# Second expert table of a PEER layer: tokens as stationary operand and 512 table columns moving, in place of table columns stationary and 384 tokens moving

## The reference, cut to what matters

```python
def one_block(xb):                       # 128 tokens
    ...                                  # eidx (T, 8, 16): ids of the chosen experts; gate: softmax of their scores
    u = u_tab[eidx]
    act = gelu(einsum('thkd,td->thk', u, xb))
    return einsum('thk,thkd->td', gate * act, v_tab[eidx])
out = x + one_block(...)                 # then the final RMSNorm
```

## Time and profile before

| | us |
|---|---|
| median of three executions | 4079.37 (4070.77 to 4085.70) |
| the profiled execution | 4075.24 |
| its span in the trace | 4073.5 |
| PE busy, share of the span | 3608.8, 89% |
| DVE busy | 2568.2, 63% |
| ACT busy | 1083.2, 27% |
| POOL busy | 1355.0, 33% |
| moved by DMA | 983.08 MB, mean 241 GB/s |

### The profile page before, as it was taken

One profiled execution on the slowest core, in us unless ns is written; L12 is line 12 of the kernel. 1 busy time (PEld: TensorE's weight loads), 2 busy tenths in 40 slices (PEclk: granted clock), 3 DMA queues, 4 the chain that ended last, 5 costly groups with the idle time before them and its releaser, 6 DMA issues. The chain is left out here.

```text
span 4073.5 us, 49975 instructions
## 1 busy us (share of the span) xinstructions
PE 3608.8 (89%) x19469; PEld 3360.9 (83%) x19469; DVE 2568.2 (63%) x3509; ACT 1083.2 (27%) x984; POOL 1355.0 (33%) x990
## 2 busy tenths in 40 slices
PE   6999996885986969987998998999599999999996
PEld 5888885664865859987998998998599999999995
DVE  4111112885213118999777777777688888898886
ACT  3222221332112213322333333332122222222222
POOL 0000000000000000111978888886154455454442
PEclk8999998776997989998999999999799999999997
DMA  4222223435323544554888989888788898989886
GB/s 161 108 108 108 108 98 109 145 120 187 132 79 140 196 156 146 218 214 172 334 332 332 345 318 354 334 318 349 289 332 334 336 353 339 357 332 357 343 328 230
DMA packets 209787, 983.08 MB, mean 241 GB/s; under 512 B 20593, under 2 KB 84401, under 8 KB 111202
## 3 DMA queue, kind: packets, MB, share of 16 engines
q1 hardware_dynamic: 130898, 523.57, 34.5%
q0 software_dynamic: 60960, 424.18, 27.2%
q10 hardware_dynamic: 17776, 33.27, 2.3%
HBM read 873.43 MB, written 107.52 MB: 241 GB/s over the span
## 5 line engine op out<-in xcount | busy, mean ns | idle before, releaser
L2062 PE MATMUL outputs_vp<-outputs_w_hi,outputs_whi 128*128 128x384 f32 x2048 | 693.0, 338 | 78.2 <-DVE outputs_w_lo L1994 41.3
L1624 PE MATMUL hidden_hp<-hidden_dense_hi,hidden_whi 128*128 128x384 f32 x2048 | 710.1, 347 | 42.0 <-DVE hidden_wlo L1408 41.9
L1625 PE MATMUL hidden_hp<-hidden_dense_lo,hidden_whi 128*128 128x384 f32 x2048 | 697.4, 341 | 0.0
L1626 PE MATMUL hidden_hp<-hidden_dense_hi,hidden_wlo 128*128 128x384 f32 x2048 | 696.5, 340 | 0.0
L2064 PE MATMUL outputs_vp<-outputs_w_hi,outputs_wlo 128*128 128x384 f32 x2048 | 691.1, 337 | 0.0
L2063 PE MATMUL outputs_vp<-outputs_w_lo,outputs_whi 128*128 128x384 f32 x2048 | 691.0, 337 | 0.0
L1553 POOL DMA_INDIRECT hidden_row<-u_rows,expert_ids x192 | 334.2, 1740 | 952.1 <-DVEq L1806 713.1
L1827 DVE CUSTOM_DVE_ANT_0 hidden_row<-hidden_row,hidden_h_row 128x2048 f32<-128x2048 f32 x192 | 439.4, 2298 | 175.2 <-DMA hidden_row<-u_rows,expert_ids 174.0
L1877 POOL DMA_INDIRECT outputs_row<-v_rows,outputs_id x192 | 321.1, 1672 | 618.9 <-DVE accg L2011 575.5
L1566 POOL TENSOR_SCALAR hidden_spare<-hidden_iota,hidden_seconds 128x128 f32<-128x128 f32 x384 | 476.1, 1252 | 122.9 <-PE hidden_tq L1609 78.2
L1404 ACT CAST outputs_whi<-outputs_raw 128x2048 fp32r<-128x2048 f32 x128 | 244.9, 1913 | 851.0 <-PE outputs_vp L2064 601.1
(11 more groups left out here) (313 smaller groups left out, 5041.4 us busy)
## 6 DMA issues: line engine op xcount, KB each, us to landing
hidden_raw<-u_units SPq DMA_DIRECT2D x128, 1024.0 KB, 8.0
outputs_raw<-v_units SPq DMA_DIRECT2D x128, 1024.0 KB, 6.5
w_in_raw<-w_in SPq DMA_DIRECT2D x48, 1024.0 KB, 5.2
hidden<-hidden_hid SPq DMA_DIRECT2D x128, 192.0 KB, 3.7
gate_mat<-hidden_big SPq DMA_DIRECT2D x12, 2048.0 KB, 14.2
outputs_w<-hidden SPq DMA_DIRECT2D x16, 1536.0 KB, 13.0
outputs_g<-gate_mat SPq DMA_DIRECT2D x16, 1536.0 KB, 21.9
w_out_raw<-w_out SPq DMA_DIRECT2D x16, 1024.0 KB, 5.7
```

Of the source, the lines that this page charges most:

```text
L1624: mm(o, un.hi[s][:, x, :], h_hi[:, x, :], start=x == 0, stop=False)
L1625: mm(o, un.hi[s][:, x, :], h_lo[:, x, :], start=False, stop=False)
L1626: ins = mm(o, un.lo[s][:, x, :], h_hi[:, x, :], start=False, stop=x == KT - 1)
L2062: mm(o, un.hi[x][:, at, :], W_hi[s][:, e, :], start=e == 0, stop=False)
```

## The change

`outputs` turns the product around. Stationary is a block of 128 tokens of the weights matrix (three blocks), moving are 512 table columns. The sums have tokens on their partitions: 3 token blocks by 2 column blocks, `GROUPS` = 6 banks at a time, for 1024 of the 2048 columns (a half). A unit of the table now holds 2 groups of experts by 1024 columns, so that four units make a half of a chunk; all six sums of a half stay open over the four units, and PE goes round the six banks once for each group of experts: 36 matmuls per unit, 512 columns moving each. A chunk is still 8 units of 1 MB with the same bytes. The half's six sums are added to `acc` in the slot of its last unit (slots 3 and 7), each by one addition of 128x512; the next half begins in the two banks that are free and needs the first of the six additions for its third. `added`, `un.done` and their waits are renumbered accordingly. PE waits for the first half of the split weights at unit 0 and for the second at unit 2, where it waited for both at unit 0.

DVE's slots hold, in order: split of unit n+1, weigh, weights_lo, gathered rows, additions. The 12 rows of a chunk are spread as 2, 2, 2, 0, 1, 2, 2, 1 over the slots.

`finish` adds `acc` directly, one 128x2048 addition per tile in place of four of 128x512 from PSUM. The transposes, the identity and its load, and PE's part are gone. The wait for the norm row moves from DVE's start to its first use. The host packs the table in the new order.

```diff
@@ outputs
+    TT, DB = ND // P, 2
+    BANKS, GROUPS = 8, ND // P * 2
+    rows_at = [0, 2, 4, 6, 6, 7, 9, 11, 12]
-        un = Units(nc, a, DT)
+        un = Units(nc, a, GROUPS)
@@ weights_hi (ACT) and weights_lo (DVE)
-                wait(act, un.done, DT * DS * (c - 1))
+                wait(act, un.done, GROUPS * DS * (c - 1))
@@ DVE
-            def add(i, s, j, b):
-                k = DT * unit(i, s, j) + b
-                vec.wait_ge(un.done, k + 1)
-                wait(vec, added, k + 1 - KT)
-                o = acc[:, DT * j + b, :]
-                v.tensor_tensor(o, o, vp[DT * (j % 4) + b][:, 0:ND], ALU.add).then_inc(added, 1)
+            def add(i, s, half, g):
+                vec.wait_ge(un.done, GROUPS * unit(i, s, 4 * half + 3) + g + 1)
+                m = GROUPS * (2 * s + half) + g
+                wait(vec, added, 4 * GROUPS * i + m + 1 - 2 * GROUPS)
+                at = (D // 2) * half + NB * (g % DB)
+                o = acc[:, g // DB, at:at + NB]
+                v.tensor_tensor(o, o, vp[m % BANKS][:], ALU.add).then_inc(added, 1)
@@ DVE body
-                        add(i, s, j, 0)
-                        for x in range(3 * (DS * s + j) // 2, 3 * (DS * s + j + 1) // 2):
-                            gathered(i, x)
-                        add(i, s, j, 1)
+                        for x in range(rows_at[j], rows_at[j + 1]):
+                            gathered(i, gat.per // 2 * s + x)
+                        if j % 4 == 3:
+                            for g in range(GROUPS):
+                                add(i, s, j // 4, g)
@@ PE body
-                        if j == 0:
-                            pe.wait_ge(w_lo_done, 2 * (2 * i + s + 1))
-                        x = j % 2
-                        for b in range(DT):
-                            wait(pe, added, DT * (n - 4) + b + 1)
-                            o = vp[DT * (j % 4) + b][:, 0:ND]
-                            for e in range(CH):
-                                at = DT * e + b
-                                mm(o, un.hi[x][:, at, :], W_hi[s][:, e, :], start=e == 0, stop=False)
-                                mm(o, un.hi[x][:, at, :], W_lo[s][:, e, :], start=False, stop=False)
-                                ins = mm(o, un.lo[x][:, at, :], W_hi[s][:, e, :], start=False, stop=e == CH - 1)
-                            ins.then_inc(un.done, 1)
+                        half, x = j // 4, j % 2
+                        if j % 2 == 0 and j < 4:
+                            pe.wait_ge(w_lo_done, 2 * (2 * i + s) + j // 2 + 1)
+                        v_hi, v_lo = (y[x][:].rearrange("p a b -> p (a b)") for y in (un.hi, un.lo))
+                        for z in range(2):
+                            e = 2 * (j % 4) + z
+                            for g in range(GROUPS):
+                                m = GROUPS * (2 * s + half) + g
+                                if e == 0:
+                                    wait(pe, added, 4 * GROUPS * i + m + 1 - BANKS)
+                                o = vp[m % BANKS][:]
+                                tok = slice(P * (g // DB), P * (g // DB + 1))
+                                at = slice((D // 2) * z + NB * (g % DB), (D // 2) * z + NB * (g % DB + 1))
+                                mm(o, W_hi[s][:, e, tok], v_hi[:, at], start=e == 0, stop=False)
+                                mm(o, W_hi[s][:, e, tok], v_lo[:, at], start=False, stop=False)
+                                ins = mm(o, W_lo[s][:, e, tok], v_hi[:, at], start=False, stop=e == CH - 1)
+                                if z == 1:
+                                    ins.then_inc(un.done, 1)
@@ finish
-            sp.dma_start(ident[:], c["ident"]).then_inc(const_in, 16)
-        @block.tensor
-        ...
-                        ins = nc.tensor.transpose(bank[b][:, k, :], acc[:, 4 * b + k, (t - 1) * P:t * P], ident[:])
-                for b in range(4):
-                    vec.wait_ge(turned, 4 * (t - 1) + b + 1)
-                    x = X[t][0:R, 512 * b:512 * (b + 1)].rearrange("p (k f) -> p k f", k=4)
-                    v.tensor_tensor(x, x, bank[b][0:R], ALU.add).then_inc(half_added, 1)
+                v.tensor_tensor(X[t][:], X[t][:], acc[:, t - 1, :], ALU.add).then_inc(summed, 1)
@@ build and kernel
-        acc, accg = sb("acc", [P, KT, ND]), ...
+        acc, accg = sb("acc", [P, ND // P, D]), ...
-        "v_units": v.reshape(NCH, CH, NKEYS, DS, DT * P).transpose(0, 3, 2, 1, 4) ...
+        "v_units": v.reshape(NCH, CH // 2, 2, NKEYS, 2, D // 2).transpose(0, 4, 1, 3, 2, 5) ...
```

More of the change, by code:

```diff
@@ L1990, in weights_lo @@
                 vec.wait_ge(w_hi_done, 2 * c + h + 1)
-                wait(vec, un.done, DT * DS * (c - 1))
+                wait(vec, un.done, GROUPS * DS * (c - 1))
                 e = slice(HC * h, HC * (h + 1))
@@ L2076, in finish @@
         junk = a.sb("junk", [P, D])
-        ident = a.sb("ident", [P, P])
         mean, root, rstd, tmp, ss = (a.sb(n, [P, TILES]) for n in ("mean", "root", "rstd", "tmp", "ss"))
-        bank = [a.ps(f"t{b}", [P, 4, P]) for b in range(4)]
         loaded = [a.sem(f"loaded{t}") for t in range(TILES)]
-        const_in, turned, summed, squared, meaned, rooted, scaled, done, stored, dstep, half_added, moved = (
-            a.sem(s) for s in ("const_in", "turned", "summed", "squared", "meaned", "rooted", "scaled", "done", "stored",
-                               "dstep", "half_added", "moved"))
+        const_in, summed, squared, meaned, rooted, done, stored, dstep, moved = (
+            a.sem(s) for s in ("const_in", "summed", "squared", "meaned", "rooted", "done", "stored", "dstep", "moved"))
         block = ctx.enter_context(nc.Block())
@@ L2098, in _ @@
             sp.wait_ge(stored, 16 * TILES)
-        @block.tensor
-        def _(pe):
-            pe.wait_ge(const_in, 32)
-            for t in range(1, PTILES):
-                for b in range(4):
-                    wait(pe, half_added, 4 * (t - 2) + b + 1)
-                    for k in range(4):
-                        ins = nc.tensor.transpose(bank[b][:, k, :], acc[:, 4 * b + k, (t - 1) * P:t * P], ident[:])
-                    ins.then_inc(turned, 1)
         @block.scalar
@@ L2115, in _ @@
                 R = rows(t)
-                if t == 0:
-                    act.wait_ge(summed, 1)
-                elif t == PTILES:
-                    act.wait_ge(summed, 3)
-                else:
-                    act.wait_ge(half_added, 4 * t)
-                if t == 0:
-                    act.wait_ge(summed, 2)
+                act.wait_ge(summed, t + 2)
                 wait(act, squared, t)
@@ L2132, in _ @@
             v, d = nc.vector, Steps(vec, dstep)
-            vec.wait_ge(const_in, 32)
             def add(t):
@@ L2157, in norm @@
                 vec.wait_ge(rooted, t + 1)
+                if t == 0:
+                    vec.wait_ge(const_in, 16)
                 newton_rsqrt(nc, d, rstd[0:R, at], mean[0:R, at], root[0:R, at], tmp[0:R, at])
@@ L2208, in build @@
                        tables["u_rows"], h_rows, expert_ids, dots, gates0, G)
-        acc, accg = sb("acc", [P, KT, ND]), [sb(f"accg{x}", [P, D]) for x in range(2)]
+        acc, accg = sb("acc", [P, ND // P, D]), [sb(f"accg{x}", [P, D]) for x in range(2)]
         outputs(nc, "outputs", tables["v_units"], hidden, G, tables["v_rows"], expert_ids, dots, acc, accg)
@@ L2255 @@
         "u_units": put("u_units", u.reshape(NKEYS, NKEYS, KT, P).transpose(0, 3, 2, 1).reshape(NKEYS, P, D)),
-        "v_units": put("v_units", v.reshape(NCH, CH, NKEYS, DS, DT * P).transpose(0, 3, 2, 1, 4).reshape(NCH * DS, P, D)),
+        "v_units": put("v_units", v.reshape(NCH, CH // 2, 2, NKEYS, 2, D // 2).transpose(0, 4, 1, 3, 2, 5).reshape(NCH * DS, P, D)),
     }
```

## The result

The changed kernel takes 4149.4 us (median of four executions, 4140.8 to 4156.0) against 4080.3 for the kernel before: ratio 1.0168, 95% interval 1.0151 to 1.0186. It is 69 us slower, where 4094 was forecast, with 4054 to 4124 as range. The profiled execution has a span of 4139.0 us, 65.5 more than before.

A forecast was written before the change was run, and what follows sets the result against it. Unit 3's arrival was taken as set by bytes in 14 of 16 chunks. Terms +21.0 (chunks 1 to 14), -2.6, -1.7, -0.9 and -1.0 gave +14.8 us, 4094 us on the median's footing, range 4054 to 4124.

The forecast's parts named there:

- What bounds the kernel: Second table: in 14 of 16 chunks the arrival of unit 3 is set by bytes, counted from load_w's issue.
- PE's rate: Second table's matmuls: 8.16 us per unit, 0.16 less than 8.32; 20.5 us for all 128 units.
- the bytes in the window behind load_w: From load_w's issue to unit 3: gathers grow from 4.2 to 4.6–4.8 MB, unit 3 comes 1.3 us later per chunk.
- Of the faster PE only 0.2 us per chunk reach the issue of load_w: From unit 3's start to the next load_w: DVE's longer slots 5 to 7 hold load_w, leaving 0.2 us gained.
- the clock, +0.4: Unit 3 behind its longer gap: more time at PE's lower clock, 0.4 us per chunk, bounds 0 and 0.9.
- the walk: Step-by-step timing of DVE's slots through one chunk from unit 3's start; DVE waits 0.6 us for a row in slot 6.
- Chunks 0 and 15, start and end: Chunks without a late load save 2.6 us, the stage's start 1.7, its end 0.9 and `finish` 1.0.
- Rival A: PE's faster rate reaches the end: 17 to 24 us saved, 4055 to 4062 us; chance 0.27.
- Rival B: PE stands 1 to 2 us in unit 4 of each chunk for late additions: 4100 to 4150 us; chance 0.13.
- Rival C: Terms cancel: gathers add nothing to the window, load_w 0.2 us earlier, clock stays; 4070 to 4084 us; chance 0.20.
- My forecast of +15 us: Whole kernel: sum of terms +14.8 us, 4094 us; own case +5 to +32 us, 4084 to 4111, chance 0.40.

The follow-up runs named there:

- experiment 4: Both kernels, from chunk 1 on loading only two of eight groups of activations and no gates: changed kernel 4022.3 us, kernel before 4023.6 us.
- (5): Both kernels with halved gathers. On 64 of 128 partitions: changed 4170.3 us, before 4081.0. At half the row width: changed 3996.3, before 4026.4.
- experiments 1: Kernel before with the change's row spread alone: 4173.0 us. Changed kernel with the old spread 1,2,1,2: 4080.9 us in one execution.
- experiment 2: Changed kernel with row 6's gather held until unit 3's high part is written: 4134.9 us; with rows spread 2,1,2,0,2,2,2,1 instead: 4141.2 us.
- Experiment 3: Kernel before with the rows of slots 6 and 7 exchanged: 4103.2 us; with those of slots 0 and 1 exchanged: 4104.8 us.

## Why the prediction was wrong

**What bounds the kernel: right.** The statement that unit 3 comes by bytes in 14 of 16 chunks is what everything turned on. Cutting the load's bytes (experiment 4) or halving the gathers' width (5) removes the gaps in both kernels.

**PE's rate: right.** 8.16 us per unit, 1049 and 1067 us bare. The fixed part of 13.3 ns that I took from the rows, and not the 2.5 ns that the Trainium skill's "TensorE: Matmul & The Clock Gate", section Back-to-back issue gap, gives for an isolated matmul, is what the changed kernel shows.

**The step that failed: the bytes in the window behind load_w, "1.3 us later" for unit 3, with bounds of 0 and 2.7 us.** The term has the right sign and place and was mis-sized: the traces have 3.5 us, above its own upper bound. The bytes account for it: at 0.39 MB per us, the mean rate in the windows of both kernels, the 1.28 MB more in the window are 3.3 us. A longer window holds more bytes whatever made it long, so this sum alone shows no cause; experiments 1, 4 and 5 do, which change the order or the load of the DMA engines and nothing of PE's work. The 1.28 MB have two parts.

The gathers brought 0.97 MB, 2.5 us, where I had 0.4 to 0.6. I had counted which gathers would be through at the time at which unit 3 used to come, and found row 4's. By the trace half of row 5's gets in as well, on average, and in the longest windows (chunks 1 and 14) all of it and part of row 6's: 6.5 MB, as much as SP's queue (6.2). That a later unit 3 lets in the next gather, and so comes later still, fits the single chunks. It isn't shown by a run of its own: with row 6's gather held back (experiment 2) the windows stayed nearly as long.

SP's queue brought 0.31 MB, 0.8 us, where I had written "the same 5.86 MB" and so put this part at nothing. They are bytes of the load of unit 4, which stands behind unit 3's in the queue: when ACT starts unit 3, 0.55 MB of it have already been moved in the kernel before, and 0.86 MB in the changed one. By their bytes the gathers alone (2.5 us) stay within my bounds; it is this part that goes over.

In five chunks ACT starts unit 3 at 25.1 to 26.2 us after the chunk's start, near my 24 to 25.5; in the others at 27.3 to 31.8. In those five the gather of row 1 is issued 3.8 to 4.0 us ahead of the chunk's start, in all others 2.5 to 2.8. What the one has to do with the other isn't settled.

**"Of the faster PE only 0.2 us per chunk reach the issue of load_w" and the clock, +0.4: both short.** From unit 3 to load_w it is +1.4 us, where the two terms gave +0.2. Of this 0.9 is the lower clock behind the longer gaps (unit 3 takes 10.24 for 8.16 us, before 9.51 for 8.32), the bound that I had named and halved. Another 0.6 is DVE, which waits 1.2 us on average for row 10 in slot 6 where the walk had 0.6. Less the 0.2 that is 1.3 of the 1.4. Experiment 3 shows in the kernel before that it is slot 6 that sets load_w: one more row there costs some 20 us.

**Two figures of the prediction were off without weight in the sum.** PE's idle time in the stretch is 1122.7 - 1085.6 = 37.1 us, not 41.1. And with load_w 1.4 us ahead of the chunk's start in place of 2.04, my own terms put PE's start of unit 3 at 29.7 us, not 29.2; it came at 32.4.

**Chunks 0 and 15, start and end: near.** 0.7 in place of 2.6 us for the two chunks, part of it a wait on an addition in unit 0 of chunk 15 (0.9 us); the start 1.7 as forecast; PE's last matmul to the end of the span 2.1 for 1.9.

**Rival A (PE's rate)** lost, for the reason given against it. **Rival B (the banks)** named a real wait in the wrong place and of little price: 13.6 us in all, 0.2 to 1.6 each, in unit 0 and none in unit 4, where unit 3's lateness hides it. **Rival C** had the terms cancel; they added up. My forecast of +15 us had the right sign and the mechanism was the one named, but at a fifth of its size; the chance of 0.29 for slower by over 20 us was too small, since it left the window's term between 0 and 2.7 us.

## What to carry to other kernels

Where a load is late by bytes and other transfers are released by the consumer's progress, the order of the consumer's work decides what gets in front of that load: spreading 12 rows as 2,2,2,0,1,2,2,1 instead of 1,2,1,2 cost 88 us with not a byte or an instruction more. A bound for such a window must let its end move, and must count the loads that stand behind the one that is waited for. The remedy was neither a faster engine nor fewer bytes but a look at due times: 0.79 MB that nobody needs for 30 us, taken from the front of the queue, gave 45 us in the kernel before.

## What the runs showed of the hardware that was not expected

A gather to 64 partitions costs the DMA engines four fifths of one to 128: 547 ns for a packet of 8 KB in place of 334, and it slows the packets beside it (384 for 335 ns). With 128 partitions and 4 KB each the relief was real: the gaps were gone.

The next load of the same queue is well under way when ACT can start on the one before it: of unit 4's 1 MB, 0.55 MB had been moved at ACT's start of unit 3 in the kernel before, 0.86 MB in the changed one, on average. Why it grew isn't shown.

PE's clock was 0.98 on average over the second table with gaps of 1.7 to 3.7 us, 0.96 with gaps of 3.0 to 10.8, and 1.00 without them. A unit behind a gap of the kernel before took 0.1 to 2.6 us longer (1.2 on average), one behind a gap of the changed kernel 1.6 to 2.8 (2.1), on top of the gap itself.
